# More even turns: how the heads of two scans and of the differential attention are woven with weight panels

## The reference

```python
# first block, differential attention: 8 heads, each with two score matrices
# a = softmax(q1 k1) - lambda * softmax(q2 k2);  out = norm(a @ v) * gain

# second block, per layer
y_ssd = _ssd_branch(s_z, s_xbc, s_dt, ...)      # 16 heads, forward and backward decay
y_hg  = _hgrn2_branch(g_q, g_f, g_i, g_g, ...)  # 8 heads of 128, forward and backward scan
y_ml  = _mlstm_branch(m_q, m_k, m_v, ...)
h = h + merged @ w_out[l]
up = _dwconv(u @ w_up[l], ffn_conv_w[l], ffn_conv_b[l])
h = h + (silu(a_half) * v_half) @ w_down[l]
```

## Time and profile before

| | us |
|---|---|
| median of 3 runs | 2515.18 |
| the 3 runs | 2522.87, 2513.99, 2515.18 |
| the profiled execution, its time | 2519.92 |
| the profiled execution, its span | 2518.1 |
| PE busy in the span | 2456.8 (98%) |
| DVE busy | 1790.1 (71%) |
| ACT busy | 1449.0 (58%) |
| mean granted clock of PE | 0.992 |

### The profile page before, as it was taken

The page is one execution under the profiler, slowest core; times in us unless marked ns, Lnnn a source line. Parts: engine busy times, 40 slices in busy tenths (PEclk is TensorE's granted clock), DMA queues, the critical chain, the costliest instruction groups (busy, mean ns, idle before and its releaser), DMA issues.

```text
span 2518.1 us, 42226 instructions
## 1 busy us (share of the span) xinstructions
PE 2456.8 (98%) x17296; PEld 2255.5 (90%) x17296; DVE 1790.1 (71%) x2897; ACT 1449.0 (58%) x2122; POOL 258.8 (10%) x222
## 2 busy tenths in 40 slices
PE   8999999999999999899999999999999999999998
PEld 8888999888889898799999799998898999899997
DVE  5567675565576755587868887885597778887875
ACT  5547555445465554477565655664766656556654
POOL 0000002000000000000113720000010106500000
PEclk9999999999999999899999999999999999999999
DMA  7543476655434566554466645555554467645663
GB/s 258 152 135 119 159 249 194 203 180 157 130 117 151 184 194 202 161 151 128 125 198 191 196 136 190 186 183 194 154 152 125 138 196 204 184 151 183 192 207 127
DMA packets 358916, 430.44 MB, mean 171 GB/s; under 512 B 20616, under 2 KB 286310, under 8 KB 358468
## 3 DMA queue, kind: packets, MB, share of 16 engines
q1 hardware_dynamic: 341312, 401.72, 51.1%
q10 hardware_dynamic: 14340, 14.93, 2.6%
q0 software_dynamic: 3072, 11.10, 1.4%
HBM read 424.44 MB, written 3.24 MB: 170 GB/s over the span
## 4 chain that ended last, share of the span: by engine, by line
PE 88%; DVE 7%; ACT 3%; issue 1%; DMA 1%; POOL 0%; POOLq 0%; ACTq 0%; DVEq 0%
PE ps L112 85%; PE ps L115 2%; DVE wlo L121 1%; ACT L118 1%; ACT hgKm L118 1%; ACT whi L118 0%; ACT E L118 0%; ACT lnv L118 0%; DVE hgQB L121 0%; DMA kT<-in_diff_lambda 0%; DVE hgQF L121 0%; DVE E L124 0%; DVE sbc L130 0%; DVE E L133 0%; DVE hgKm L121 0%
## 5 line engine op out<-in xcount | busy, mean ns | idle before, releaser
L121 DVE TENSOR_TENSOR wlo<-wring,whi 128x1024 fp32r<-128x1024 f32 (+1 forms) x768 | 920.2, 1218 | 257.0 <-ACT whi L118 256.2
L118 ACT ACTIVATE whi<-wring 128x1024 fp32r<-128x1024 f32 (+1 forms) x768 | 802.8, 1054 | 431.3 <-PE ps L112 405.2
L112 PE MATMUL ps<-uT,whi 128*128 128x256 f32 x4640 | 822.2, 281 | 6.7 <-DVE wlo L121 5.0
L112 PEld LDWEIGHTS ps<-uT,whi 128*128 128x128 f32 x4640 | 706.7, 188 | 16.1 <-DVE wlo L121 8.2
L112 PE MATMUL ps<-uT,wlo 128*128 128x256 f32 x2320 | 646.8, 279 | 0.0
L112 PEld LDWEIGHTS ps<-uT,wlo 128*128 128x128 f32 x2320 | 438.9, 189 | 0.0
L112 PE MATMUL ps<-xT,whi 128*128 128x256 f32 x2112 | 378.1, 283 | 2.5 <-DVE xT L121 1.3
L112 PEld LDWEIGHTS ps<-xT,whi 128*128 128x128 f32 x2112 | 321.8, 188 | 10.2 <-issue 6.2
L112 PE MATMUL ps<-xT,wlo 128*128 128x256 f32 x1056 | 294.6, 279 | 0.0
L112 PE MATMUL ps<-whi,hid 128*128 128x512 f32 x864 | 270.4, 392 | 1.6 <-DVE wlo L121 1.6
L112 PEld LDWEIGHTS ps<-xT,wlo 128*128 128x128 f32 x1056 | 198.2, 188 | 0.3
(11 more groups left out here) (395 smaller groups left out, 3570.6 us busy)
## 6 DMA issues: line engine op xcount, KB each, us to landing
wring<-in_w_in SPq DMA_DIRECT2D x346, 512.0 KB, 4.2
wring<-in_mlp_w SPq DMA_DIRECT2D x128, 512.0 KB, 4.3
wring<-in_w_up SPq DMA_DIRECT2D x88, 512.0 KB, 4.5
wring<-in_w_down SPq DMA_DIRECT2D x44, 512.0 KB, 4.4
wring<-in_w_branch SPq DMA_DIRECT2D x32, 512.0 KB, 3.3
wring<-in_w_out SPq DMA_DIRECT2D x32, 512.0 KB, 4.5
wring<-in_mem_w_kv SPq DMA_DIRECT2D x16, 512.0 KB, 6.3
wring<-in_w_br_hg SPq DMA_DIRECT2D x16, 512.0 KB, 5.2
```

What stands on the lines that cost most here:

```text
L112: return self.e.matmul(*p, **k) if self.e else Nothing()
L118: return self.e.activation(*p, **k) if self.e else Nothing()
L121: return self.e.tensor_tensor(*p, **k) if self.e else Nothing()
```

## The change

1. `hg`: the second half's `hg_scan` gets three of its turns (start and split; first product; level 0's merge, scale and products) inside the last turns of the first half. The first half has 24 turns at 1.22 against `by_panels(hg_proj(1))` at 1. `by_panels` takes a turn only when a new panel was emitted, so that the output of a block no longer has a turn of its own. The remaining 18 turns of the second half go at 1.1 against the 16 panels of `two_gates` at 1.
2. `hg`: merge j+1 waits for each scaled tensor by itself (QF, kf, kb on ACT, QB on POOL) and no longer for the whole of scale j. The copy of the first product into `hgA` moves from DVE to ACT (`hg_first`). In `hg_proj` g is made ahead of v, and the last `forget_scale` comes after g's first panel.
3. SSD: with `steady=True` every iteration has two turns (45 in all), and the 24 panels of `ml_proj` go by panels at 0.55 to 1.
4. Differential attention: one more turn ahead of the pipeline, and with `even=True` the stages that have not begun yet take their turns too (53 turns).
5. Feed-forward: the last `ffn_product` comes after the first two panels of `w_down`.

```diff
-def staged(n, *stages):
+def staged(n, *stages, even=False, steady=False):
...
                 f(i - lag)
-                if rest or i >= n:
+                if rest or i >= n and not steady:
                     yield
+            elif rest and (steady or even and i < lag):
+                yield
...
+    def by_panels(g):
+
+        n = len(panels)
+        for _ in g:
+            if len(panels) > n:
+                n = len(panels)
+                yield
...
+            yield
             yield from staged(8, (scores(0), 0, True), (scores(1), 0, True), (lambda h: turn_unit(un[h, 0]), 1, True), (values, 2, True),
-                              (norm, 3, False), (weights, 0, False), (gain, 4, False))
+                              (norm, 3, False), (weights, 0, False), (gain, 4, False), even=True)
...
+            B.g = ar.take("hgg", 1024, at=o + 6144)
+            to_g = projB(w, GG + c0, 512, uT, features_to(B.g, ACT.Silu))
+            next(to_g)
+            do("forget_scale", *pend.pop())
+            yield
+            yield from to_g
...
+            do("hg_first", B, us)
             yield
-            do("hg_level", B, -1, us)
...
-            yield
+            if not hf:
+
+                some(following, 1)
+                yield
+
...
-            W.sq = Slots([Buf("hgsq", 0, 512, W.QK[0][1].ap[:, o:o + 512]) for o in (0, 512)])
+
+            W.sq = [Slots([Buf("hgsq", 0, 512, b.ap[:, o:o + 512]) for o in (0, 512)]) for b in (B0.kf, W.QK[0][1])]
...
-            yield from staged(16, (exponents, 0, True), (decays, 1, False), (weights, 2, False), (outputs, 3, False), (norms, 4, True))
+            yield from staged(16, (exponents, 0, True), (decays, 1, False), (weights, 2, False), (outputs, 3, False), (norms, 4, True), steady=True)
...
-        weave((hg_scan(0, B0, W), 1), (hg_proj(1, B1), 1.3))
+        second = hg_scan(1, B1, W)
+        weave((hg_scan(0, B0, W, second), 1.22), (by_panels(hg_proj(1, B1)), 1))
...
-        weave((hg_scan(1, B1, W), 1), (two_gates(), 1))
+        weave((second, 1.1), (by_panels(two_gates()), 1))
...
-        weave((ssd_scan(), 1), (ml_proj(), 1.0))
+
+        weave((ssd_scan(), 1), (by_panels(ml_proj()), 0.55))
...
+        down = projA(a["w_down_2"][l], 0, 1024, hid, add_to_h(("h2", l)))
+
+        some(down, 2)
         do("ffn_product", hid, *f.wait)
         ar.give(uT, fc, *aslots, *vslots)
-        down = projA(a["w_down_2"][l], 0, 1024, hid, add_to_h(("h2", l)))
-        some(down, 14)
+        some(down, 12)
...
         if j >= 1:
             e.wait_ge(*at(("hgprod", B.tag, j - 2)))
-            e.wait_ge(*at(("hgscaled", B.tag, j - 1)))
+            e.wait_ge(*at(("hgscaled", B.tag, j - 1, "QF")))
...
+    def hg_first(B, us):
+
+        if B.last:
+            e.wait_ge(*at(("yhraw", B.last, 2)))
+        for st in range(2):
+            e.wait_ge(*at(us[st].full))
+            e.activation(B.W.A4[:, st, :, st * 128:st * 128 + 128], us[st].ap.rearrange("p (h t) -> p h t", h=4), ACT.Copy).then_inc(
+                *up("act_hg", us[st].key, ("hglevel", B.tag, st, -1)))
...
     def hg_start(B):
         if B.last:
-            e.wait_ge(*at(("yh", B.c.l, B.hf * 4 - 1)))
+            e.wait_ge(*at(("hgprod", B.last, 6)))
```

More of the change, by code:

```diff
@@ L1000, in hg_proj, with hg_scan @@
             yield from projB(w, GF + 1024 + c0, 512, uT, forget(B.b, B.kb, 8 + hf * 4))
+            B.g = ar.take("hgg", 1024, at=o + 6144)
[4 more added lines that the diff above has]
+            yield from to_g
             B.v = ar.take("hgv", 1024, at=o + 5120)
             yield from projA(w, GI + c0, 512, uT, tokens_to(B.v, 512))
[L1003 to L1007, removed]
+        def hg_scan(hf, B, W, following=None):
             B.tag, B.c, B.hf, B.sq = ("hg", l, hf), c, hf, {}
@@ L1032, in hg_scan @@
             yield
-            yield
+            if not hf:
+                some(following, 1)
+                yield
             def values(h):
-                B.sq[h] = W.sq.take()
+                B.sq[h] = W.sq[hf].take()
                 do("hg_values", B, c, h, AB.take(), yh)
@@ L1567, in hg_cross @@
                 m = e.matmul(p3[:, h, :], k4[:, h, st * 128:st * 128 + 128], q4[:, h, 128 - st * 128:256 - st * 128], start=True, stop=True)
-            m.then_inc(*up("pe_level", u.full))
+            m.then_inc(*up("pe_level", u.full, *([("hgcross", B.tag)] if st else [])))
     def hg_values(B, c, h, u, yh):
@@ L1911, in hg_merge @@
         e.activation(halves(Qm, 1, n), halves(B.W.QF, 1, n), ACT.Copy).then_inc(*up("act_hg", ("hgQF", B.tag, j)))
+        if j >= 1:
+            e.wait_ge(*at(("hgscaled", B.tag, j - 1, "kf")))
         e.activation(halves(Km, 0, n), halves(B.kf, 0, n), ACT.Copy)
+        if j >= 1:
+            e.wait_ge(*at(("hgscaled", B.tag, j - 1, "kb")))
         e.activation(halves(Km, 1, n), halves(B.kb, 1, n), ACT.Copy).then_inc(*up("act_hg", ("hgK", B.tag, j)))
+    def hg_first(B, us):
[5 more added lines that the diff above has]
+                *up("act_hg", us[st].key, ("hglevel", B.tag, st, -1)))
     def hg_cross(B, us):
@@ L2041, in scalar_program @@
                  merged=merged, ln_stats=ln_stats, ln_out=ln_out, relu_square=relu_square, square_part=square_part, square_rows=square_rows, rms_scale=rms_scale, small_gates=small_gates,
-                 cumsum_rows=cumsum_rows, store_rows=store_rows, store_max=store_max, spread_rows=spread_rows, ml_max_cols=ml_max_cols, forget_out=forget_out, hg_merge=hg_merge, hg_cross=hg_cross,
+                 cumsum_rows=cumsum_rows, store_rows=store_rows, store_max=store_max, spread_rows=spread_rows, ml_max_cols=ml_max_cols, forget_out=forget_out, hg_merge=hg_merge, hg_first=hg_first, hg_cross=hg_cross,
                  hg_values=hg_values, hg_norm=hg_norm, ssd_conv=ssd_conv, ssd_silu=ssd_silu, ssd_turn=ssd_turn,
@@ L2486, in hg_split @@
         W = B.W
+        if B.last:
+            e.wait_ge(*at(("hgcross", B.last)))
         for k in (0, 2):
@@ L2499, in hg_scale @@
         e.wait_ge(*now("dve_hg"))
-        for x, side, T, ev in ((W.QF, 1, Tf, "hgQF"), (B.kf, 0, Tf, "hgK"), (W.QB, 0, Tb, "hgQB"), (B.kb, 1, Tb, "hgK")):
+        for x, side, T, ev, name in ((W.QF, 1, Tf, "hgQF", "QF"), (B.kf, 0, Tf, "hgK", "kf"), (W.QB, 0, Tb, "hgQB", "QB"), (B.kb, 1, Tb, "hgK", "kb")):
             e.wait_ge(*at((ev, B.tag, j)))
-            o = e.tensor_tensor(half(x, side), half(x, side), tb(T, 1 - side), ALU.mult)
+            e.tensor_tensor(half(x, side), half(x, side), tb(T, 1 - side), ALU.mult).then_inc(*up("dve_hg", ("hgscaled", B.tag, j, name)))
         if j < 6:
             e.tensor_tensor(W.Tf[j % 2].ap[:, 0:nb], tp(Tf, 0), tp(Tf, 1), ALU.mult)
-            o = e.tensor_tensor(W.Tb[j % 2].ap[:, 0:nb], tp(Tb, 0), tp(Tb, 1), ALU.mult)
-        o.then_inc(*up("dve_hg", ("hgscaled", B.tag, j)))
+            e.tensor_tensor(W.Tb[j % 2].ap[:, 0:nb], tp(Tb, 0), tp(Tb, 1), ALU.mult).then_inc(*up("dve_hg"))
     def hg_rows(B, c, h, yh):
@@ L2761, in hg_merge @@
             e.wait_ge(*at(("hgprod", B.tag, j - 2)))
-            e.wait_ge(*at(("hgscaled", B.tag, j - 1)))
+            e.wait_ge(*at(("hgscaled", B.tag, j - 1, "QB")))
         else:
```

7 lines of the change are left out of this document (1 added, 6 removed).

## The result

| | before | after |
|---|---|---|
| median of 4 runs each, us | 2517.15 | 2498.64 |
| ratio, 95% interval | | 0.9924 [0.9903, 0.9946] |
| the profiled execution, its time | 2519.92 | 2502.51 |
| the profiled execution, its span | 2518.1 | 2500.7 |
| mean granted clock of PE | 0.992 | 0.993 |

The change makes the kernel 18.5 us faster by the medians (19.1 by the ratio), where 20.4 was forecast. The measured 2498.6 lies 3.8 us above the forecast of 2494.8 and in its range; 2.0 of the 3.8 are the median of before, which was 2515.18 of three runs and is 2517.15 of four. The page's first part of the kernel after, which answers to rows 1: PE has 3.8 us less busy time with the same 17296 matmuls, and 47.7 us of the span are left idle.

What follows compares the result with a forecast made beforehand. PE, busy 2456.8 of 2518.1 us, was taken as the bound, so only its idle or half-clock time could be won. Terms 11.9 + 6.0 + 1.9 + 0.6 = 20.4 us, off the 2515.2 median, gave 2494.8 us, range 2485 to 2510.

Steps and rivals of the forecast that it cites:

- hg scans: hg scans, both layers: 14.9 us of PE idle and half clock, less 3.0 kept back, gives 11.9 us gained.
- attention: Differential attention: waits on the second head's softmax and layer 1's half clock go, 6.0 us gained (bounds 0 and 6.2).
- feed-forward: The first down panel's wait for `wlo` behind the product goes in both layers, 1.9 us gained (bounds 0 and 2).
- SSD: SSD, both layers: 3.7 us of end waits go, 3.0 us of new costs come, 0.6 us gained.
- The 0.17 us to be added to each idle in brackets: PE's shown idles are 0.17 us short, since a single matmul is shown that much longer than its spacing.
- The four waits and the half clock: hg scans, layer 0: PE idles of 0.69, 0.22, 1.59, 2.57 us plus 1.7 for half clock; 14.9 us for both layers.
- The 3.0 us that I kept back: hg scans: 1.5 us a layer left for nearly full ACT in the first half's tail, taken off 14.9.
- The first half's waits: hg levels 2 and 3: 0.69 and 0.22 us, blamed on ACT's merge; events per tensor would end its copies some 2 us earlier.
- the second half's burst: hg second half's start: waits of 1.59 and 2.57 us from work queued on DVE and ACT, cured by starting it earlier.
- DVE just holds: SSD middle: DVE falls 0.35 us a head behind over 12 heads, 4.2 us, within its two-panel lead of 5.4.
- POOL's pace: Rival, chance 0.14: POOL sets the SSD's pace at 4.26 us a head, costing 5.1 us a layer; 2501.9 us.
- the exclusion of DVE and POOL: Rival, chance 0.08: DVE and POOL lock each other out in the SSD, costing 8.8 us a layer; 2509.3 us.

Runs made afterwards that it cites:

- whole_scale: The kernel after, with merge j+1 waiting for the last operation of all of scale j again: 2497.55 us, ratio 0.9917.
- panels_only: The kernel before, with only the first half's hg panels spread evenly over its scan: 2515.47 us in one run.
- first_only: The kernel before, with only the copy of the hg scan's first product moved from DVE to ACT: 2511.43 us in one run.
- late_gain_2: The kernel after, with DVE's gain multiplies of the SSD's norm in their own step two iterations later, second run: 2494.41 us, ratio 0.9906.
- ssd_only: The kernel before, with the SSD's even turns alone: 2519.49 us, ratio 1.0012.
- attn_ffn_only: The kernel before, with the attention's extra turns and the moved feed-forward product alone: 2510.68 us, ratio 0.9975.
- after_old_ssd_2: The kernel after, with the SSD's turns as before, second run, on another chip: 2494.46 us, ratio 0.9908.

## Why the prediction was right, step by step

The forecast was right in time, and in three of four terms by size. Two errors of some 4 us offset each other, so that the sum came out this close is luck. In us, with the ledger of the profile after:

| term | forecast | ledger |
|---|---|---|
| hg scans | -11.9 | -15.5 |
| attention | -6.0 | -5.1 |
| feed-forward | -1.9 | -2.1 |
| SSD | -0.6 | +3.8 |
| sum | -20.4 | -18.9 (the medians say -18.5) |

- **What bounds the kernel** held: PE is at 98% before and after, and only its idle and half-clock time moved. The 0.17 us to be added to each idle in brackets held where a plain panel stands ahead (0.79 shown is 0.95 from start to start beyond the usual spacing). It was too small for the attention's wait, where 2.07 shown is 2.33, so the prediction had that term 0.1 us short each time.
- **hg, size.** The four waits and the half clock were worth the whole 14.9 us that I counted and 0.6 more. The 3.0 us that I kept back for a tight tail of ACT were the mis-sized part: ACT is busy 25.39 of 29 us there, as worked out (about 26 of 29), and yet PE waits for nothing. A full ACT costs only if something that PE needs soon stands behind it.
- **hg, mechanism.** Half wrong. The first half's waits were put on the merge standing behind all of the scale. whole_scale shows that the events add nothing, and panels_only and first_only that either the spread or the moved copy removes the waits. I had dismissed the spread ("turns change little there") by the mean number of panels a turn; what counts is the round that has two panels in it. For the second half's burst I credited the overlap with everything. It gives 2.1 to 2.5 us a layer; the moved copy, which I had counted only as a load on ACT, gives as much in the second half (2.0 to 2.1) and 1 us more in the first.
- **Attention** held, at 5.1 for 6.0, though 1.7 of it is the half clock behind layer 1's wait, which kernels with the same wait show in the other layer, in both or not at all, so that this part is luck: without it the term is 4.3 forecast and 3.4 found, 1.7 a layer. The second head's wait shrank to 0.49 us in both layers rather than to nothing, and one of 0.16 came behind it.

```profile
184.79 0.85 PE L115 MATMUL ps<-cst,E 128*128 128x128 f32 x4 [0.49 <-DVE E L130]
192.34 0.85 PE L115 MATMUL ps<-cst,E 128*128 128x128 f32 x4 [0.16 <-DVE E L130]
```

- **Feed-forward** held: the first down panel of the kernel after follows the last up-projection with no wait, where rows 12 have 0.81.

```profile
1679.57 0.28 PE L112 MATMUL ps<-uT,wlo 128*128 128x256 f32 x1
1679.69 0.39 PE L112 MATMUL ps<-whi,hid 128*128 128x512 f32 x1
```

- **SSD** failed, in the step "DVE just holds": -0.6 us forecast, +3.8 in the ledger. The working of DVE's rate (3.75 to 3.8 us a head against 3.45) left 1.2 us of lead over 12 heads, and left out DVE's one wait of 2.87 us for ACT's norm. It stood in the trace of before, at 1400.09, and DVE's own waits in that stretch would have shown it. Put into the sum, 4.2 + 2.87 is 7.1 against a lead of 5.4, 1.7 us a layer short; the two waits at 1391.90 and 1397.30 are 0.95 and 1.63, together 2.58. But the sum itself does not hold. DVE does not fall behind by 0.35 us a head: in the kernel after `wlo` is ready 6.3 us ahead of its panel at 1356.53, 1.6 at 1368.96 and 4.4 at 1388.09, just ahead of the wait, and in late_gain_2, without the wait, it stays 2.7 to 4.2 us ahead from 1369.53 to 1399.86. The step that failed is the wait that was left out, with what stands behind it on DVE. (The prediction's 3.7 - 3.0 is 0.7, where it has 0.6.) The point that I had named as proof against me, over 2 us a layer of waits for `wlo` or the weights in the middle heads, came true (2.2 in layer 0), by a mechanism that was none of the rivals.
- **POOL's pace** as a rival is ruled out. In 1355 to 1415 us of the kernel after POOL's groups are

```profile
L124 POOL TENSOR_SCALAR sE<-mxb,sm 128x256 f32<-128x256 f32 x18 | 28.1, 1568 | 10.3 <-DMA mxb<-spread 6.7 <-PE ps L112 3.6
L124 POOL TENSOR_SCALAR sE<-rows,sm 128x256 f32<-128x256 f32 x10 | 19.5, 1959 | 0.4 <-DMA rows<-spread 0.4
```

which is 47.6 us for 28 operations, 3.4 a head (the prediction asked for below 3.6), and POOL still idles. DVE's `sE` multiply takes 940 to 959 ns beside POOL's 914 to 3085, as in rows 11. So the exclusion of DVE and POOL is not seen in DVE's durations here either. What the Trainium skill states on it (SBUF — State Buffer, "SBUF: two separate sides") can show in POOL's durations, and no run tells how much of them it is.

## What to carry to other kernels

When panels are spread more thinly beside a scan, go through every wait of the engine whose lead shrinks, also those on helpers that cost nothing before: here one wait of 2.87 us on ScalarE's norm turned the gain of a whole edit into a loss, and moving its consumer two steps later gave it back. Look at what stands behind the wait and when it is due, and not only at the lead when the wait begins, which was the same before and after. Here moving one piece of 1.28 us off the crowded engine did as much for a burst of work as overlapping it with the part before. And when several edits are made together, try each alone before you credit one: two of them cured the same wait, and a third that was written for it did nothing.

## What was not expected of the hardware

**Dense matmuls have two spacings.** Plain panels of 256 columns start 113.3 or 117.7 ns apart, for whole stretches, at a granted clock of 1.00 in both. The first up-projection of layer 0, before, then after (columns as in rows 4):

```profile
1590.00:1680.00 90.00, 90.00 (x766) 90.00 (x766) 74.27 (x113) 56.45 (x80) 0.00 (x0) 1.00 0.59 188
```

```profile
1580.00:1660.00 80.00, 80.00 (x709) 80.00 (x708) 68.78 (x104) 52.62 (x75) 0.00 (x0) 1.00 0.62 190
```

That is 117.5 and 112.8 ns a matmul with none idle. The spacing changes at panel borders and differs between two profiles of the same program. It adds some 20 to 29 us to every run, an estimate that takes each interval of the looser kind, also of 512 columns, less the closer spacing; no cause was found. It is as large as the whole effect studied here and averages out between before and after only by luck (some 26 and 25 us in their profiles).

**Half clock follows long idle, but not always at the same place.** The hg scans' wait of 2.4 to 2.6 us stands twice in each of before, ssd_only, panels_only and attn_ffn_only, and behind seven of the eight the granted clock fell to 0.50 or 0.52 (rows 4, panels_only above); behind the one in layer 1 of attn_ffn_only, shown above, it stayed at 1.00. Behind 1.2 + 0.7 us and behind 0.6 it stayed at 1.00 too. Behind the attention's wait of 2.33 to 2.42 us it fell in four of ten places. Here is ssd_only behind both of its waits, layer 0 then layer 1:

```profile
188.20:191.60 3.40, 3.40 (x18) 3.40 (x18) 2.84 (x6) 2.98 (x11) 0.00 (x0) 0.53 0.15 51
697.30:700.70 3.40, 3.40 (x29) 3.21 (x30) 3.33 (x7) 2.39 (x9) 0.00 (x0) 1.00 0.38 133
```

Other stretches at 0.50, at places with nothing changed, came and went between profiles: before has one at 561.8 us, which after_old_ssd_2 lacks, and the one that begins at 1039.6 us and lasts 13.7 there begins at 1030.6 and lasts 6.8 in after_old_ssd_2. What sets this apart was not found.
